# Splitting the projection weights of the second attention at other steps of a head

## The chip, the cores and the metric

The program runs on one core of one Trainium2 chip. The metric is the device time of one execution in microseconds; the median of three runs is given.

## The reference

Two encoder layers over 1024 frames of 1024 features, in float32. Layer 0 uses differential attention with 8 heads, layer 1 latent attention (MLA) with 16 heads; each is followed by a squared-ReLU MLP. The change lies in layer 1's attention: queries come from a 512-wide latent, keys and values from a 256-wide one, 32 of a head's 96 query features are rotated by position, and block t of 128 queries sees the keys up to its own block.

```python
def _rms_norm(x, w):
    xf = x.astype(F32)
    y = xf * lax.rsqrt(jnp.mean(xf * xf, axis=-1, keepdims=True) + RMS_EPS)
    return (y * w.astype(F32)).astype(x.dtype)
...
def mla_attention(u, pos, w_down, q_norm_w, w_uq, kv_norm_w, w_ukv, w_o):
    B, S, _ = u.shape
    down = u @ w_down
    c_q = _rms_norm(down[..., :MLA_Q_LORA], q_norm_w)
    c_kv = _rms_norm(down[..., MLA_Q_LORA:MLA_Q_LORA + MLA_KV_LORA], kv_norm_w)
    k_rope = _rope(down[..., MLA_Q_LORA + MLA_KV_LORA:][:, :, None, :], pos)[:, :, 0]
    q = (c_q @ w_uq).reshape(B, S, MLA_HEADS, MLA_NOPE + MLA_ROPE)
    q_nope = q[..., :MLA_NOPE]
    q_rope = _rope(q[..., MLA_NOPE:], pos)
    kv = (c_kv @ w_ukv).reshape(B, S, MLA_HEADS, MLA_NOPE + MLA_V)
    k_nope, v = kv[..., :MLA_NOPE], kv[..., MLA_NOPE:]
    scale = (MLA_NOPE + MLA_ROPE) ** -0.5
    outs = []
    for qb in range(S // Q_BLOCK):
        q0 = qb * Q_BLOCK
        n_keys = q0 + Q_BLOCK
        s = (jnp.einsum('bqhd,bkhd->bhqk', q_nope[:, q0:n_keys], k_nope[:, :n_keys])
             + jnp.einsum('bqhr,bkr->bhqk', q_rope[:, q0:n_keys], k_rope[:, :n_keys])).astype(F32) * scale
        p = _masked_softmax(s, _chunk_mask(q0, n_keys)[None, None])
        outs.append(jnp.einsum('bhqk,bkhe->bqhe', p.astype(v.dtype), v[:, :n_keys]))
    o = jnp.concatenate(outs, axis=1)
    return o.reshape(B, S, MLA_HEADS * MLA_V) @ w_o
...
    for i in range(DEPTH):
        ...
            y = mla_attention(u, pos, mla_w_down[j], mla_q_norm_w[j], mla_w_uq[j],
                              mla_kv_norm_w[j], mla_w_ukv[j], mla_w_o[j])
        x = _layer_norm(DEEPNORM_ALPHA * x + (1.0 + g1) * y, ln_g[i, 0], ln_b[i, 0])
        u = x * (1.0 + sc2) + sh2
        y = squared_relu_mlp(u, ffn_w1[i], ffn_w2[i])
        x = _layer_norm(DEEPNORM_ALPHA * x + (1.0 + g2) * y, ln_g[i, 1], ln_b[i, 1])
```

## The kernel before

Every float32 product is made of three matmuls in a reduced float format: both operands are held as a high part (the value rounded to the format) and a low part (what is left), and high x high, high x low and low x high are added (`SPLIT`). Activations are kept split. Weights come from HBM by DMA into one of two slots of `raw` and are split there: ScalarE copies the slot into the high half of `W` (`split_hi`, L683), VectorE subtracts that from `raw` and writes the low half (`split_lo`, L1102). Weights have a running number g; its parity is the slot. PE waits for `w_lo`, the count of finished splits, before a product. ScalarE waits for the DMA and for PE to be done with the slot; SyncE loads the next slab into a slot of `raw` when its `w_lo` is reached.

The second attention takes its 16 heads one after another, heads 0 and 1 and heads 14 and 15 written out, heads 2 to 13 as six turns of a loop with two heads each. All engines walk through `heads1(h0, i, last)`, which has eight steps s = 0 to 7, one for each block of 128 queries; they are called the first to the eighth step below, and heads are numbered from 0. Their order of work is written out by hand in this function, once for each engine, and semaphores tie the engines together.

In step s of head h PE turns the exponentials of block s (`turn1`, L1658, 128x128 transposes into `TB` or the bank PA1), makes the scores of the block two steps on (`scores1`, L1980), and in odd s one piece of the next head's projections (`proj1`, by `product`, L1651): queries for the first 512 frames (s = 1, 12 matmuls), keys and values for the first 512 (s = 3, 6 matmuls), queries (s = 5) and keys and values (s = 7) for the second 512. All four pieces use one PSUM bank, `PA[0]`, so that each waits until VectorE has emptied the one before (`qk_evac`). In s = 2, 4, 6 and at the start of the next head it makes the value products of a pair of blocks (`values1`, L2013, then two transposes, L2016). In s = 0 it also turns the values of the head (`turn_v`, L2000 and L1658).

ScalarE makes the exponentials (`exp1`, L1028), the high parts of the turned blocks (`p_hi`, `v_hi`, L729) and of the projections (`copy_piece`, L1019 and L1021), and copies outputs (L1042, L769). VectorE takes row maxima (`max1`, L1566), reciprocals (`inverse1`, L1572), low parts of turned blocks (`p_lo`, `v_lo`, L1184) and of projections (`lo_piece`: L1549 for keys; L1556, L1557 and L1559 for queries), and finishes outputs (`sum_out`: L1586, L1588, then L1230). GpSimd rotates the queries (`rope_q`, L652 to L654), on `tmp`, when VectorE has written it (L1557). SyncE stores outputs and loads weights: in head h the query weights (512 rows, with two small loads of swapped columns) and the key and value weights (256 rows) of head h + 2.

The weights of head h + 1 are split during head h: the query weights (512 columns of `W`) in the first step, the key and value weights (256 columns) in the third, each as the last operation of that step on ScalarE and on VectorE:

```python
                    if proj and s == 0:
                        split_lo(g0, 2 * i, QT)
                    if proj and s == 2:
                        split_lo(g0 + 1, 2 * i, KVT)
```

`proj` is true for heads 0 to 14. `values1` waits for VectorE's earlier outputs (`o_fin`), for the reciprocals, and for the low parts of all blocks it reads (`t_evac`):

```python
                pe.wait_ge(a1["o_fin"], 4 * h + pair)
                pe.wait_ge(a1["l_inv"], NQ * h + last + 1)
                pe.wait_ge(a1["t_evac"], 13 * h + group_of(last, 1 if last >= 4 else 0) + 1)
```

Of the kernel before, what the change touches and what calls it, by code (L numbers as in the profile page):

```python
# [36 lines left out]
QT, KVT = Q_LORA // P, KV_LORA // P  # L37
# [49 lines left out]
def group_of(s, part):  # L87

    return part + (0 if s == 0 else s + 1 + max(0, s - 4))


def is_first(h):

    return isinstance(h, int) and h == 0
# [29 lines left out]
def encoder(nc, x, c, pos_offset, ada_w, ada_b, ln_g, ln_b, rel_table, w_qkv, w_o0, lq1, lk1, lq2,  # L124
# [3 lines left out]
    with ctx:  # L128
# [547 lines left out]
        def _(act):  # L676
            def split_hi(g0, hi, kt, products, count):

                slot = g0 % 2
                act.wait_ge(w_in[slot], 16 * (g0 // 2 + hi + 1))  # L680
                if products is not None:
                    act.wait_ge(products, count)
                nc.scalar.activation(W[:, slot, 0, 0:kt * P], raw[:, slot, 0:kt * P], ACT.Copy).then_inc(w_hi, 1)  # L683
# [81 lines left out]
            def out_hi(s, h, pair, rows, src):  # L765
                act.wait_ge(s["o_fin"], 4 * h + pair + 1)
                if not (isinstance(h, int) and h == 0 and pair == 0):
                    act.wait_ge(s["o_stored"], 16 * (4 * h + pair))
                nc.scalar.activation(ostage[0:rows, 0, :].bitcast(F32R), src, ACT.Copy).then_inc(s["o_hi"], 1)  # L769
# [180 lines left out]
            def split_uq(g0, hi, h, products, count):  # L950
                act.wait_ge(swap_in[0], 32 * h + 64)
                split_hi(g0, hi, QT, products, count)
# [58 lines left out]
            a1 = HS[1]  # L1011
# [32 lines left out]
            def heads1(h0, i, last=False):  # L1044
                h, p = h0 + 2 * i, h0 % 2
                proj = not (last and h0 % 2)
                g0 = G_HEADS1 + 2 * (h0 + 1)
                for s in range(NQ):
                    if s + 1 < NQ:
                        exp1(h, s + 1)  # L1050
                    elif proj:
                        exp1(h + 1, 0)
                    if s == 1:
                        v_hi(h, p)
                    p_hi(h, p, s, 0)
                    if s >= 4:
                        p_hi(h, p, s, 1)
                    if s == 0 and not is_first(h):
                        copy_piece(p, h, 3, PA[0])
                    if s in (2, 4, 6) and proj:  # L1060
                        copy_piece(1 - p, h + 1, s // 2 - 1, PA[0])
                    if s == 1 and not is_first(h):
                        out_bottom(h - 1, 3)
                        out_hi(a1, h - 1, 3, VD, osum[0:VD, :])
                    if s in (3, 5, 7):
                        out_bottom(h, (s - 3) // 2)
                        out_hi(a1, h, (s - 3) // 2, VD, osum[0:VD, :])
                    if proj and s == 0:
                        split_uq(g0, 2 * i, h + 1, a1["pj_ready"], 4 * h + 3)
                    if proj and s == 2:  # L1070
                        split_hi(g0 + 1, 2 * i, KVT, a1["pj_ready"], 4 * h + 4)
                    if not proj and s == 0:
                        split_hi(G_WO1, 0, KT, a1["pj_ready"], 4 * HEADS1)

# [20 lines left out]
        def _(dve):  # L1095
            own = Seq(dve, dve_seq)

            def split_lo(g0, hi, kt):

                slot = g0 % 2  # L1100
                dve.wait_ge(w_hi, g0 + 2 * hi + 1)
                nc.vector.tensor_tensor(W[:, slot, 1, 0:kt * P], raw[:, slot, 0:kt * P],  # L1102
                                        W[:, slot, 0, 0:kt * P].bitcast(F32), ALU.subtract).then_inc(w_lo, 1)
# [438 lines left out]
            a1 = HS[1]  # L1542
# [40 lines left out]
            def sum_out(h, pair):  # L1583
                dve.wait_ge(a1["o_sq"], 4 * h + pair + 1)
                dve.wait_ge(a1["o_lo"], 4 * h + pair)
                nc.vector.tensor_tensor(osum[0:VD, :], VB[0:VD, 0:PAIR], obot[0:VD, :], ALU.add).then_inc(a1["o_sum"], 1)  # L1586
                dve.wait_ge(a1["o_sum"], 4 * h + pair + 1)
                nc.vector.tensor_tensor(osum[0:VD, :], osum[0:VD, :], VB[0:VD, PAIR:2 * PAIR], ALU.mult)\  # L1588
                    .then_inc(a1["o_fin"], 1)
                out_lo(a1, h, pair, VD, osum[0:VD, :])  # L1590

            def heads1(h0, i, last=False):
                h, p = h0 + 2 * i, h0 % 2
                proj = not (last and h0 % 2)
                g0 = G_HEADS1 + 2 * (h0 + 1)
                for s in range(NQ):
                    inverse1(h, s)
                    if s == 1:
                        v_lo(h, p)
                    p_lo(h, p, s, 0)  # L1600
                    if s + 2 < NQ:
                        max1(h, s + 2)
                    elif proj:
                        max1(h + 1, s + 2 - NQ)
                    if s >= 4:
                        p_lo(h, p, s, 1)
                    if s == 0 and not is_first(h):
                        lo_piece(p, h, 3, PA[0])
                    if s in (2, 4, 6) and proj:
                        lo_piece(1 - p, h + 1, s // 2 - 1, PA[0])  # L1610
                    if s == 1 and not is_first(h):
                        sum_out(h - 1, 3)
                    if s in (3, 5, 7):
                        sum_out(h, (s - 3) // 2)
                    if proj and s == 0:
                        split_lo(g0, 2 * i, QT)
                    if proj and s == 2:
                        split_lo(g0 + 1, 2 * i, KVT)
                    if not proj and s == 0:
                        split_lo(G_WO1, 0, KT)  # L1620

# [22 lines left out]
        def _(pe):  # L1644
# [311 lines left out]
            a1 = HS[1]  # L1956
# [48 lines left out]
            def values1(h, pair):  # L2005
                last = 2 * pair + 1
                pe.wait_ge(a1["o_fin"], 4 * h + pair)
                pe.wait_ge(a1["l_inv"], NQ * h + last + 1)
                pe.wait_ge(a1["t_evac"], 13 * h + group_of(last, 1 if last >= 4 else 0) + 1)
                for j in range(last + 1):  # L2010
                    c0 = 0 if j < last else P
                    for b in (1, 0):
                        ins = mm(VB[:, c0:PAIR], V1[:, j, :], at1(pair)[:, b, j, c0:PAIR], start=j == 0 and b == 1,  # L2013
                                 stop=j == last and b == 0)
                for k in range(2):
                    ins = nc.tensor.transpose(VB[0:VD, PAIR + k * P:PAIR + (k + 1) * P],  # L2016
                                              row_inv(2 * pair + k).to_broadcast([P, VD]), ident)
                ins.then_inc(a1["o_ready"], 1)
# [94 lines left out]
```

## Time and profile before

| | |
|---|---|
| median of 3 runs | 3080.66 us (3074.52 to 3080.73) |
| profiled execution | 3074.19 us |
| its span | 3072.5 us |
| PE busy | 2708.4 us, 88% of the span |
| VectorE (DVE) busy | 1689.0 us, 55% |
| ScalarE (ACT) busy | 1184.6 us, 39% |
| GpSimd (POOL) busy | 336.0 us, 11% |
| mean granted PE clock | 0.949 of full speed |

Busy times are of the whole span, which has several stages: setup and the first attention, its output product, the first MLP, the latents, the second attention (from about 1704 to about 2220 us), its output product, the second MLP and the end. The profile names instructions by engine and line, the chain is the work that ended last followed back, and a wait is put down to the engine that released it. Durations of neighbouring instructions on VectorE and ScalarE overlap by some hundredths of a microsecond, so that the distance from one start to the next is a little shorter than the duration.

### The profile page before, as it was taken

Reading aid. Unit: us, or ns where it says so; the run is one execution under the profiler, and the core shown is the slowest. Engines: PE = TensorE matmul, PEld = TensorE weight load, DVE = VectorE, ACT = ScalarE, POOL = GpSimd, SP = SyncE. Lnnn points to the kernel's source line nnn. Section 1 sums busy time; section 2 is a strip of 40 time slices with the busy share of each in tenths; the row PEclk is TensorE's granted clock in tenths of the full one; section 3 lists DMA queues with packets and bytes.
Section 4 is the critical chain, followed back from the end, with each engine's and each line's share of the span. In section 5 each row is a group of like instructions: output and inputs, shape, how many; then the busy total and the mean of one; then the engine's idle time right before and its main releaser. Section 6 shows DMA issues by size and latency. Waiting matters only on the chain.

```text
span 3072.5 us, 37975 instructions
## 1 busy us (share of the span) xinstructions
PE 2708.4 (88%) x12716; PEld 2231.9 (73%) x12716; DVE 1689.0 (55%) x2888; ACT 1184.6 (39%) x2125; POOL 336.0 (11%) x362
## 2 busy tenths in 40 slices
PE   1678878887999999999998788888789999999996
PEld 1566666665778888888776677777567888888884
DVE  3466666665575444354375777777558323232346
ACT  0355555554262120312255565665426212131223
POOL 2000000000020001016032322222101000000000
PEclk9789998886999999999999999999899999999997
DMA  6422222223434324142233111111353211111122
GB/s 195 143 68 73 70 69 66 64 59 145 150 95 130 103 69 135 44 129 61 71 115 86 21 32 27 27 32 26 128 159 86 77 48 48 48 48 48 48 82 76
DMA packets 331200, 245.78 MB, mean 80 GB/s; under 512 B 41000, under 2 KB 303447, under 8 KB 331103
## 3 DMA queue, kind: packets, MB, share of 16 engines
q1 hardware_dynamic: 314062, 185.82, 20.7%
q0 software_dynamic: 17040, 58.73, 6.3%
q8 instruction: 53, 0.87, 0.1%
q14 instruction: 45, 0.36, 0.0%
HBM read 215.12 MB, written 33.59 MB: 81 GB/s over the span
## 4 chain that ended last, share of the span: by engine, by line
PE 63%; DVE 13%; ACT 10%; issue 9%; DMA 4%; ACTq 0%; DVEq 0%; POOL 0%; SPq 0%; POOLq 0%
PE PA L1651 31%; PE SC L1651 24%; PE VB L1739 3%; DVE H L1184 2%; DVE soft L1566 2%; ACT H L729 2%; ACT X L745 2%; DMA ada<-in_ada_w 1%; DVE W L1102 1%; ACT X L1028 1%; ACT W L683 1%; PE TB L1658 1%; DVE H L1223 1%; ACT H L723 1%; DVE X L1588 1%
## 5 line engine op out<-in xcount | busy, mean ns | idle before, releaser
L1651 PE MATMUL PA<-U,W 128*128 128x512 f32 x3840 | 948.8, 402 | 80.8 <-DVE W L1102 46.9
L1651 PEld LDWEIGHTS PA<-U,W 128*128 128x128 f32 x3840 | 730.6, 192 | 245.5 <-issue 57.7
L683 ACT ACTIVATE W<-raw 128x1024 fp32r<-128x1024 f32 (+2 forms) x262 | 259.8, 992 | 830.9 <-PE PA L1651 389.9
L1651 PE MATMUL SC<-U,W 128*128 128x512 f32 x2064 | 484.2, 394 | 4.4 <-DVE W L1102 4.2
L1651 PEld LDWEIGHTS SC<-U,W 128*128 128x128 f32 x2064 | 389.5, 189 | 91.5 <-DVE W L1102 5.9
L1102 DVE TENSOR_TENSOR W<-raw,W 128x1024 fp32r<-128x1024 f32 (+2 forms) x262 | 313.8, 1198 | 99.6 <-ACT W L683 97.9
L1651 PE MATMUL PA<-H,W 128*128 128x512 f32 x1536 | 358.7, 393 | 3.2 <-DVE W L1102 3.2
L1651 PE MATMUL SC<-H,W 128*128 128x512 f32 x1536 | 354.4, 390 | 0.0
L1651 PEld LDWEIGHTS PA<-H,W 128*128 128x128 f32 x1536 | 288.6, 189 | 64.3 <-DVE W L1102 3.6
L1651 PEld LDWEIGHTS SC<-H,W 128*128 128x128 f32 x1536 | 288.5, 188 | 60.5 <-issue 1.0
L729 ACT ACTIVATE H<-TB 128x512 fp32r<-128x512 f32 (+3 forms) x216 | 107.8, 499 | 217.0 <-PE TB L1658 215.6
L1184 DVE TENSOR_TENSOR H<-TB,H 128x512 fp32r<-128x512 f32 (+3 forms) x216 | 122.5, 567 | 122.2 <-ACT H L729 121.8
L1350 DVE SCALAR_TENSOR_TENSOR X<-PA,aff,X 128x512 f32 (+1 forms) x80 | 60.0, 750 | 211.3 <-PE PA L1651 211.3
L1350 DVE SCALAR_TENSOR_TENSOR X<-SC,aff,X 128x512 f32 (+1 forms) x80 | 60.0, 750 | 202.4 <-PE SC L1651 190.1
L524 POOL DMA_DIRECT2D ada<-in_ada_w x96 | 68.8, 717 | 918.8 <-DVE acc L1116 914.3
L1658 PE MATMUL TB<-cst,X 128*128 128x128 f32 (+1 forms) x712 | 124.7, 291 | 48.8 <-DVE H L1184 31.1
L1739 PE MATMUL VB<-H 128*128 128x256 f32 (+1 forms) x480 | 92.8, 371 | 69.9 <-DVE H L1184 69.6
L1739 PEld LDWEIGHTS VB<-H 128*128 128x128 f32 x480 | 90.3, 284 | 74.4 <-DVE H L1184 39.9
L1658 PEld LDWEIGHTS TB<-cst,X 128*128 128x128 f32 (+1 forms) x712 | 86.7, 150 | 74.8 <-issue 21.8
L1980 PE MATMUL SC<-H 104*128 104x512 f32 (+3 forms) x576 | 140.3, 372 | 0.0
L1116 DVE SCALAR_TENSOR_TENSOR acc<-ada,cact,acc 128x512 f32<-128x512 f32 x168 | 125.9, 750 | 23.7 <-DMA ada<-in_ada_w 19.5
L1436 DVE SCALAR_TENSOR_TENSOR tmp<-PA,tmp 128x512 f32<-128x512 f32 x64 | 44.2, 691 | 169.7 <-ACT tmp L892 169.7
(209 smaller groups left out, 2984.1 us busy)
## 6 DMA issues: line engine op xcount, KB each, us to landing
raw<-in_ffn_w SPq DMA_DIRECT2D x160, 512.0 KB, 4.1
ada<-in_ada_w POOLq DMA_DIRECT2D x96, 512.0 KB, 4.7
U<-attention_out SPq DMA_DIRECT2D x4, 3584.0 KB, 17.4
raw<-in_da_w_qkv SPq DMA_DIRECT2D x24, 512.0 KB, 4.2
attention_out<-ostage SPq DMA_DIRECT2D x32, 256.0 KB, 2.7
raw<-in_da_w_o SPq DMA_DIRECT2D x16, 512.0 KB, 4.1
X<-residual SPq DMA_DIRECT2D x4, 2048.0 KB, 11.6
attention_out<-ostage SPq DMA_DIRECT2D x64, 128.0 KB, 2.3
```

Source lines behind the costliest of these rows:

```text
L524: pool.dma_start(ada[:, u % 2, :, :], src[:, 2 * u:2 * u + 2, bass.ds(b * BW, BW)]).then_inc(ada_in[u % 2], 16)
L683: nc.scalar.activation(W[:, slot, 0, 0:kt * P], raw[:, slot, 0:kt * P], ACT.Copy).then_inc(w_hi, 1)
L729: nc.scalar.activation(hi_dst, src, ACT.Copy).then_inc(s["t_hi"], 1)
L745: nc.scalar.activation(w, w, ACT.Exp, bias=st[:, 4 + comp:5 + comp], accum_out=st[:, 6 + comp:7 + comp]).then_inc(a0["p_ready"], 1)
L1102: nc.vector.tensor_tensor(W[:, slot, 1, 0:kt * P], raw[:, slot, 0:kt * P], W[:, slot, 0, 0:kt * P].bitcast(F32), ALU.subtract).then_inc(w_ ...
L1116: ins = nc.vector.scalar_tensor_tensor(acc[:, :], src, by, acc[:, :], ALU.mult, ALU.add)
L1184: nc.vector.tensor_tensor(dst, src, hi_ap.bitcast(F32), ALU.subtract).then_inc(s["t_evac"], 1)
L1350: nc.vector.scalar_tensor_tensor(tile, bank, by, tile, ALU.mult, ALU.add).then_inc(d_evac, 1)
L1651: ins = mm(bank, W[:, slot, a, kt * P:(kt + 1) * P], moving(b, kt)[:, cols], start=kt == first and (a, b) == SPLIT[0], stop=kt == last and ...
L1658: return nc.tensor.transpose(out_ap, in_ap, ident[r0:r0 + n, r0:r0 + n])
L1739: ins = mm(VB[:, c0:PAIR], V0[:, a, j, :], AT0[:, b, j, c0:PAIR], start=j == 0 and (a, b) == SPLIT[0], stop=j == last and (a, b) == SPLIT[-1])
L1980: ins = mm(SC[s % 2][:, k], q1(p, a)[0:MR.stop, s * P:(s + 1) * P], k1(p, b)[0:MR.stop, k], start=(a, b) == SPLIT[0], stop=(a, b) == SPLIT ...
```

## The change

On ScalarE and VectorE alike, in the second attention:

- the key and value weights of the next head are split in the first step instead of the third;
- the query weights are split in the seventh step, two heads ahead: in head h those of head h + 2, in heads 0 to 13;
- head 0 in addition splits the query weights of head 1 in its first step, as before.

ScalarE's copy in the seventh step waits for the two swapped loads of that slab and for the second query product of head h + 1, which PE made in the sixth step. On PE, `values1` waits for the low parts in two portions: for blocks 0 to 3 ahead of the first matmul, for blocks 4 to 7 ahead of the fifth block. No operation is added or left out but these waits: the sequence of splits as such, by number, is the same, and SyncE's instructions are the same.

```diff
--- before.py
+++ after.py
@@ -1065,10 +1065,12 @@
                     if s in (3, 5, 7):
                         out_bottom(h, (s - 3) // 2)
                         out_hi(a1, h, (s - 3) // 2, VD, osum[0:VD, :])
+                    if is_first(h) and s == 0:
+                        split_uq(g0, 2 * i, h + 1, a1["pj_ready"], 4 * h + 3)
                     if proj and s == 0:
-                        split_uq(g0, 2 * i, h + 1, a1["pj_ready"], 4 * h + 3)
-                    if proj and s == 2:
                         split_hi(g0 + 1, 2 * i, KVT, a1["pj_ready"], 4 * h + 4)
+                    if not last and s == 6:
+                        split_uq(g0 + 2, 2 * i, h + 2, a1["pj_ready"], 4 * h + 7)
                     if not proj and s == 0:
                         split_hi(G_WO1, 0, KT, a1["pj_ready"], 4 * HEADS1)
 
@@ -1612,10 +1614,12 @@
                         sum_out(h - 1, 3)
                     if s in (3, 5, 7):
                         sum_out(h, (s - 3) // 2)
+                    if is_first(h) and s == 0:
+                        split_lo(g0, 2 * i, QT)
                     if proj and s == 0:
-                        split_lo(g0, 2 * i, QT)
-                    if proj and s == 2:
                         split_lo(g0 + 1, 2 * i, KVT)
+                    if not last and s == 6:
+                        split_lo(g0 + 2, 2 * i, QT)
                     if not proj and s == 0:
                         split_lo(G_WO1, 0, KT)
 
@@ -2006,8 +2010,9 @@
                 last = 2 * pair + 1
                 pe.wait_ge(a1["o_fin"], 4 * h + pair)
                 pe.wait_ge(a1["l_inv"], NQ * h + last + 1)
-                pe.wait_ge(a1["t_evac"], 13 * h + group_of(last, 1 if last >= 4 else 0) + 1)
                 for j in range(last + 1):
+                    if j % 4 == 0:
+                        pe.wait_ge(a1["t_evac"], 13 * h + group_of(last, j // 4) + 1)
                     c0 = 0 if j < last else P
                     for b in (1, 0):
                         ins = mm(VB[:, c0:PAIR], V1[:, j, :], at1(pair)[:, b, j, c0:PAIR], start=j == 0 and b == 1,
```

What this does to VectorE's order, shown for head 1, which is written out. In the changed kernel VectorE's line numbers are 2 higher. The third step before, from the row maxima of block 4 on (L1566):

```order
L1566 TENSOR_REDUCE soft<-SC 128x1
L1556 SCALAR_TENSOR_TENSOR tmp<-PA,ada 32x512
L1557 SCALAR_TENSOR_TENSOR tmp<-PA,ada 32x512
L1559 SCALAR_TENSOR_TENSOR H<-PA,H 64x512
L1102 TENSOR_TENSOR W<-raw,W 128x256
L1572 RECIPROCAL soft<-soft 128x1
L1184 TENSOR_TENSOR H<-PA,H 128x4x128
```

and now:

```order
L1558 SCALAR_TENSOR_TENSOR tmp<-PA,ada 32x512
L1559 SCALAR_TENSOR_TENSOR tmp<-PA,ada 32x512
L1561 SCALAR_TENSOR_TENSOR H<-PA,H 64x512
L1574 RECIPROCAL soft<-soft 128x1
L1186 TENSOR_TENSOR H<-PA,H 128x4x128
L1568 TENSOR_REDUCE soft<-SC 128x1
```

The split has gone from between L1559 (now L1561) and the reciprocal that opens the fourth step. The seventh step's end and the eighth step before:

```order
L1556 SCALAR_TENSOR_TENSOR tmp<-PA,ada 32x512
L1557 SCALAR_TENSOR_TENSOR tmp<-PA,ada 32x512
L1559 SCALAR_TENSOR_TENSOR H<-PA,H 64x512
L1572 RECIPROCAL soft<-soft 128x1
L1184 TENSOR_TENSOR H<-TB,H 128x4x128
L1566 TENSOR_REDUCE soft<-SC 128x1
L1184 TENSOR_TENSOR H<-PA,H 128x4x128
L1586 TENSOR_TENSOR X<-VB,X 64x256
L1588 TENSOR_TENSOR X<-X,VB 64x256
```

and now:

```order
L1558 SCALAR_TENSOR_TENSOR tmp<-PA,ada 32x512
L1559 SCALAR_TENSOR_TENSOR tmp<-PA,ada 32x512
L1561 SCALAR_TENSOR_TENSOR H<-PA,H 64x512
L1104 TENSOR_TENSOR W<-raw,W 128x512
L1574 RECIPROCAL soft<-soft 128x1
L1186 TENSOR_TENSOR H<-TB,H 128x4x128
L1568 TENSOR_REDUCE soft<-SC 128x1
L1186 TENSOR_TENSOR H<-PA,H 128x4x128
L1588 TENSOR_TENSOR X<-VB,X 64x256
L1590 TENSOR_TENSOR X<-X,VB 64x256
```

The split of 512 columns now stands between the same two kinds of operation as the one of 256 did in the third step. The first step's end, before and now:

```order
L1184 TENSOR_TENSOR H<-PA,H 128x128
L1566 TENSOR_REDUCE soft<-SC 128x1
L1549 TENSOR_TENSOR H<-PA,H 64x512
L1102 TENSOR_TENSOR W<-raw,W 128x512
L1572 RECIPROCAL soft<-soft 128x1
L1184 TENSOR_TENSOR H<-TB,H 128x8x64
```

```order
L1186 TENSOR_TENSOR H<-PA,H 128x128
L1568 TENSOR_REDUCE soft<-SC 128x1
L1551 TENSOR_TENSOR H<-PA,H 64x512
L1104 TENSOR_TENSOR W<-raw,W 128x256
L1574 RECIPROCAL soft<-soft 128x1
L1186 TENSOR_TENSOR H<-TB,H 128x8x64
```

There 256 columns are split in place of 512. ScalarE's order changes in the same way: its copy stands last in the same steps.

## Rows read from the trace of the kernel before

**Rows 1.** Page, part 4: the chain that ended last, by engine.

```profile
PE 63%; DVE 13%; ACT 10%; issue 9%; DMA 4%; ACTq 0%; DVEq 0%; POOL 0%; SPq 0%; POOLq 0%
```

**Rows 2.** Waits, 1736 to 2180 us: engine, line, waited for; total us, times, longest.

```profile
PE PA L1651 <- DVE W L1102: 33.2, 14, 2.5
...
PE PA L1651 <- DVE H L1559: 15.8, 14, 1.2
```

**Rows 3.** Chain that ended last, 1928 to 1993 us: start us, us, what.

```profile
1969.25 1.22 DVE W L1102
...
1988.83 0.42 DVE X L1588
```

**Rows 4.** Timeline of PE, one head: start us, us, instruction, [idle before].

```profile
1957.86 2.11 PE L2013 MATMUL VB<-H 128*128 128x256 f32 x16 [0.25 <-DVE X L1588]
...
1960.39 0.60 PE L1658 MATMUL PA<-cst,X 64*128 64x64 f32 x7
...
1970.60 1.65 PE L1651 MATMUL PA<-U,W 128*128 128x512 f32 x6 [2.34 <-DVE W L1102]
```

**Rows 5.** Timeline of DVE, the same head.

```profile
1960.80 0.67 DVE L1102 TENSOR_TENSOR W<-raw,W 128x512 fp32r<-128x512 f32 x1
...
1969.25 1.22 DVE L1102 TENSOR_TENSOR W<-raw,W 128x256 fp32r<-128x256 f32 x1
1970.39 0.14 DVE L1572 RECIPROCAL soft<-soft 128x1 f32<-128x1 f32 x1
...
1986.81 0.14 DVE L1572 RECIPROCAL soft<-soft 128x1 f32<-128x1 f32 x1
...
1988.83 0.41 DVE L1588 TENSOR_TENSOR X<-X,VB 64x256 f32<-64x256 f32 x1
...
1992.41 0.67 DVE L1102 TENSOR_TENSOR W<-raw,W 128x512 fp32r<-128x512 f32 x1
```

**Rows 6.** Timeline of ACT, the same head.

```profile
1960.07 0.62 ACT L683 ACTIVATE W<-raw 128x512 fp32r<-128x512 f32 x1
1960.59 0.56 ACT L1028 ACTIVATE X<-SC,soft 128x384 f32<-128x384 f32 x1
...
1961.14 0.58 ACT L729 ACTIVATE H<-PA 128x512 fp32r<-128x512 f32 x1
...
1966.23 0.41 ACT L683 ACTIVATE W<-raw 128x256 fp32r<-128x256 f32 x1
...
1989.36 0.42 ACT L769 ACTIVATE ostage<-X 64x256 fp32r<-64x256 f32 x1 [2.87 <-DVE X L1588]
```

**Rows 7.** Timeline of POOL, the same head.

```profile
1968.69 1.50 POOL L652 TENSOR_TENSOR H<-tmp 32x512 fp32r<-32x512 f32 x1 [10.07 <-DVE tmp L1557]
...
1986.25 1.26 POOL L652 TENSOR_TENSOR H<-tmp 32x512 fp32r<-32x512 f32 x1 [13.29 <-DVE tmp L1557]
```

**Rows 8.** Groups of DVE by form, 1700 to 2222 us.

```profile
L1102 DVE TENSOR_TENSOR W<-raw,W 128x256 fp32r<-128x256 f32 x15 | 18.3, 1220 | 0.0
...
L1102 DVE TENSOR_TENSOR W<-raw,W 128x1024 fp32r<-128x1024 f32 x1 | 1.2, 1226 | 0.3 <-ACT W L683 0.3
```

**Rows 9.** Timeline of DVE, head 0, first and third step.

```profile
1706.28 1.14 DVE L1102 TENSOR_TENSOR W<-raw,W 128x512 fp32r<-128x512 f32 x1
...
1712.81 0.56 DVE L1184 TENSOR_TENSOR H<-PA,H 128x384 fp32r<-128x384 f32 x1 [3.32 <-ACT H L729]
```

**Rows 10.** Timeline of POOL, head 0, first step.

```profile
1705.60 1.27 POOL L654 TENSOR_TENSOR H<-tmp,H 32x512 fp32r<-32x512 f32 x1
```

**Rows 11.** Windows of 1 us: us, busy by engine, PEclk, DMA share, GB/s.

```profile
1782.30:1783.30 1.00, 1.00 (x6) 1.00 (x5) 0.44 (x3) 0.84 (x2) 0.21 (x1) 0.50 0.00 0
```

**Rows 12.** Timeline of DVE, first-step split of a later head.

```profile
2024.23 0.67 DVE L1102 TENSOR_TENSOR W<-raw,W 128x512 fp32r<-128x512 f32 x1
```

**Rows 13.** Timeline of PE, heads 10 and 15.

```profile
2034.02 2.92 PE L1651 MATMUL PA<-U,W 128*128 128x512 f32 x6 [2.33 <-DVE W L1102]
...
2217.41 3.68 PE L2013 MATMUL VB<-H 128*128 128x256 f32 x16 [2.18 <-DVE X L1588]
```

## The prediction

> **What bounds the kernel now.** I read the page's chain that ended last first. It is PE for 63% of the span [rows 1], but that is a mean over stages, and the change lies in one of them alone, the second attention. So I went to the waits of that stage. Per head PE sits idle 33.2 / 14 = 2.37 us before the first key and value product, until VectorE has written the low part of the weights (L1102), and 15.8 / 14 = 1.13 us before the second such product, until VectorE has emptied the only projection bank (L1559) [rows 2]. A reader who stops here sees 2.4 us of PE per head to be won. The chain cut to this stage says otherwise: it runs over VectorE and ScalarE, and both the split of the third step and the last VectorE operation of the eighth, L1588, are links of it [rows 3]. PE waits at both ends; it does not set the pace.
>
> One head takes 1992.41 - 1960.80 = 31.61 us from first-step split to first-step split [rows 5]. What must be seen in the three timelines: the third-step split delays VectorE by 1970.39 - 1969.25 = 1.14 us [rows 5] and PE starts only behind it [rows 4]. After the seventh step's L1559, VectorE goes on at 1986.81 and runs without a gap to L1588 at 1988.83 [rows 5]; ScalarE has then been idle for 2.87 us and starts at once when L1588 is done [rows 6], and so does PE with the last value product [rows 4]. Everything of the next head hangs on that moment. So a split put behind L1559 in the seventh step delays the next head by its full length.
>
> **The change, part by part**, against the profiled execution (3074.19 us, of which 3072.5 is span; it lies 6.5 us under the median of the three runs, and I carry the difference over to the median).
>
> Third step, heads 0 to 14: the 256-column split goes away. VectorE is 1.14 us earlier from there on, and the softmax work behind it (L1184, L1566, L1586, L1588) finds its inputs ready. PE gains about as much, not 2.37, since the bank is free only after L1559, which stands right ahead of the split. 15 x -1.14 = **-17.1 us**.
>
> First step, heads 1 to 14: 256 columns are split in place of 512. ScalarE's copy of 512 pushes the next operation back by 1960.59 - 1960.07 = 0.52 us; that of 256 is 0.62 - 0.41 = 0.21 shorter [rows 6]. Only part of that counts: L729 at 1961.14 needs the value transposes, which PE ends at 1960.39 + 0.60 = 1960.99 [rows 4]. With some 0.04 us for the hand-over, 0.11 us are left. The bounds are 0 and 0.21; I take 0.11, since the ends are near each other. 14 x -0.11 = **-1.5 us**. In head 0 both splits stand in the first step; the second one costs nothing on the path, because VectorE has 3.32 us to spare two steps on, where ScalarE and PE are late [rows 9]. Without that cover it would cost about 0.3 us, once.
>
> Seventh step, heads 0 to 13: the 512-column split comes behind L1559. ScalarE's half (0.52 us) delays its exponential of the next head, but VectorE is held much longer and ends last. The low half is an operation with two inputs in SBUF, and GpSimd works at the same moment. In the third step GpSimd's L652 starts at 1968.69 and the split 0.56 us behind it; the split of 256 columns takes 1.22 us there [rows 5, 7], 15 times out of 15 [rows 8], against 0.67 for 512 columns where GpSimd rests [rows 5]. In the seventh step the new split would start at 1986.81, again 0.56 us behind an L652, at 1986.25 [rows 5, 7]: the same geometry. 256 columns more cost (1.23 - 0.67) / 2 = 0.28 us [rows 5, 8], so I expect 1.14 + 0.28 = 1.42 us of delay. Below, 0.60 us would be the price if nothing held it (0.67 less the overlap of some 0.07 that the third-step rows show between length and step); above, 1.14 + 2 x 0.28 = 1.70 if the held part grows with the columns as well. I take 1.42, built on the row with the same neighbour at the same distance. 14 x 1.42 = **+19.9 us**.
>
> A rule speaks here too. Head 0's first-step split shows the holding: it takes 1.14 us and ends at 1707.42, 0.55 us behind the end of L654 at 1706.87 [rows 9, 10]. The Trainium skill (SBUF — State Buffer, Who interferes with whom) says that a VectorE instruction with two SBUF inputs and a GpSimd instruction that reads SBUF take turns, and that whoever came first keeps the shared port for its whole instruction. By that the new split would end 0.55 us behind an L652 of 1.26 us, a delay of 0.70 + 0.55 - 0.08 = 1.17 us, and the sum would come out 14 x 0.25 = 3.5 us lower. Head 0 agrees with the rule, the third step doesn't quite: there L652 itself grows to 1.50 us and the split ends 0.24 us later than in turn [rows 5, 7]. The row decides for me.
>
> The divided wait in the value products: I cost it at nothing. On VectorE each L1588 stands behind both halves of the same step's weights, and PE waits for L1588 (its count of finished outputs) at the head of the same function. So the early half never lets PE start earlier. It adds two waits a head to PE; if each took 0.03 us on the path it would be 14 x 0.03 = 0.4 us for the one that matters. The DMAs keep their order on SyncE; the query weights are issued in the second step of a head and are needed five steps on, and the load of the key and value weights is no longer held until the third step.
>
> PE's clock: in eight of the 15 heads the product after the 2.4 us wait runs partly at the lower level (granted 0.50, that is 1.2 GHz [rows 11]; 2.92 us against 1.65 [rows 4, 13]), and such a head takes 2024.23 - 1992.41 = 31.82 us [rows 5, 12], 0.21 more. The idle time there shrinks to about 1.2 us, and no fall follows the waits of 1.13 us in the old seventh step. I take 8 x -0.21 = **-1.7 us**; the other bound is 0.
>
> Sum: -17.1 - 1.5 + 19.9 - 1.7 = **-0.4 us**: the stall moves from the third step to the turn of the head, and the price is about the same. 3080.66 - 0.4 = **3080.2 us**. About 0.2% (6.2 us) is what a measurement of this kernel can tell from no change.
>
> **Rivals.**
> The split is not held in the seventh step, or the third-step gain is larger than I see: at 0.60 us of delay the sum falls by 14 x 0.82 = 11.5 us, to 3069. For it: GpSimd shows only 1.26 us for this L652. Against it: the distance of 0.56 us is fixed by the same three VectorE operations. If VectorE's eighth step had slack after all, the whole seventh-step term would go, and the time would be near 3060; the gapless run to L1588 speaks against that.
>
> The clock falls at the turn of the head (the slower side). PE now waits 1.1 us for L1559, then about 0.4 for the weights of the eighth step, then about 1.1 for L1588: some 2.6 of 5.2 us idle, where the old third step had 2.4 in one piece. If the clock falls there, it hits the value product, behind which the transposes have only 0.04 us of slack left. The row at the lower level is 3.68 against 2.11 us [rows 4, 13], so 1.6 us per fall. In 7 of 14 heads that is +11 us: 3091. It decides from the fifth such head on. For it: in the last head, where PE has no projections and many waits, that product did run at the lower level [rows 13]. Against: each piece is shorter than the 1.13 us pieces that did no harm.
>
> The held part doubles (1.70): 14 x 0.28 = +3.9 us, 3084, no change that can be told.
>
> The change does nothing at all for PE: that can't be, the splits do change places.
>
> **How the numbers follow.** My forecast, no change, with the doubled holding and the rule's 3.5 us in it: 0.55. Split not held, or slack in the eighth step: 0.24, faster. Clock at the turn, with what else of waiting I miss: 0.21, slower. The forecast's own range is 3075 to 3086 (the rule's and the doubled price, with the scatter of the runs). To leave out no more than 2 in 10 it must reach to both neighbours: 3068 to 3091. Faster by over 0.2%: 0.24; within: 0.55; slower: 0.21.
>
> **What would show it.** Right: PE's wait before the first key and value product falls to about 1.2 us and is put down to L1559; the 512-column split takes about 1.5 us in 14 heads, with L652 at 1.5 us before it; PE waits some 1.1 us for L1588 ahead of the last value product and 0.4 us ahead of the first transposes of the next head; a head takes 31.4 to 31.9 us. Wrong: seventh-step splits of 0.67 us, heads under 31.2 us, or a granted clock of 0.50 in the value product that opens a head.

## The result and the profile after

| | before | changed |
|---|---|---|
| median, 20 runs each | 3074.05 us | 3088.94 us |
| lowest and highest | 3062.27 to 3086.77 | 3072.55 to 3098.81 |
| profiled execution, its span | 3074.19, 3072.5 | 3079.43, 3077.7 |
| mean granted PE clock | 0.949 | 0.952 |

The ratio is 1.0052, 95% interval 1.0038 to 1.0065: **slower**, by about 16 us (12 to 20). The forecast was no change: -0.4 us against before, whose median of 20 runs is 3074.05 in place of the 3080.66 of three.

The stage of the change, from head 0's first-step split to head 15's split of 1024 columns, took 476.53 us before and takes 485.73 us now: +9.2 us. The two profiled spans differ by only 5.2 us, because what lies ahead of the stage was 4 us shorter in that execution: the stage began at 1702.26 us and not at 1706.28. So +9.2 us is what the trace of one execution shows inside the stage, and 16 us is the difference of the medians.

First the waits of PE in the second attention, heads 1 to 14, changed kernel, as in [rows 2]:

```profile
PE PA L1655 <- DVE H L1561: 29.1, 27, 1.2
PE VB L2018 <- DVE X L1590: 13.3, 14, 1.0
PE TB L1662 <- DVE H L1186: 12.4, 21, 0.8
PE PA L1662 <- DVE H L1186: 11.7, 20, 0.7
```

The 33.2 us on the split are gone, and both key and value products now wait 1.0 to 1.1 us for the bank. New are 13.3 us ahead of the value products (1.8 before) and longer waits ahead of the transposes (3.1 and 3.1 before). The four groups sum to 66.5 us; the same four and the split summed to 57.0 us before. So the wait that PE lost has come back at other places, and more than that.

Next the turn of one head, timelines of VectorE and GpSimd, to be held against [rows 5, 7]:

```profile
1954.64 0.68 DVE L1561 SCALAR_TENSOR_TENSOR H<-PA,H 64x512 fp32r<-64x512 f32 x1
1955.25 1.77 DVE L1104 TENSOR_TENSOR W<-raw,W 128x512 fp32r<-128x512 f32 x1
1956.95 0.15 DVE L1574 RECIPROCAL soft<-soft 128x1 f32<-128x1 f32 x1
...
1958.98 0.41 DVE L1590 TENSOR_TENSOR X<-X,VB 64x256 f32<-64x256 f32 x1
...
1962.55 0.41 DVE L1104 TENSOR_TENSOR W<-raw,W 128x256 fp32r<-128x256 f32 x1
```

```profile
1954.69 1.78 POOL L652 TENSOR_TENSOR H<-tmp 32x512 fp32r<-32x512 f32 x1 [12.43 <-DVE tmp L1559]
1956.55 1.60 POOL L653 TENSOR_TENSOR tmp<-tmp 32x512 f32<-32x512 f32 x1
1958.23 1.26 POOL L654 TENSOR_TENSOR H<-tmp,H 32x512 fp32r<-32x512 f32 x1
```

The split stands where it was expected, 0.56 us behind the start of an L652, but it takes 1.77 us, in 14 heads of 14 (1.77 or 1.78), and delays VectorE by 1956.95 - 1955.25 = 1.70 us. L652 takes 1.78 us, not the 1.50 that I expected.

And PE at the turn of a head; the first fence is a head like most, the second one of four:

```profile
1955.38 1.67 PE L1655 MATMUL PA<-U,W 128*128 128x512 f32 x6 [1.13 <-DVE H L1561]
1957.74 0.33 PE L1662 MATMUL TB<-cst,X 128*128 128x128 f32 x1 [0.69 <-DVE H L1186]
1957.83 0.77 PE L1984 MATMUL SC<-H 104*128 104x384 f32 x3
1959.62 2.12 PE L2018 MATMUL VB<-H 128*128 128x256 f32 x16 [1.02 <-DVE X L1590]
```

```profile
1857.82 1.66 PE L1655 MATMUL PA<-U,W 128*128 128x512 f32 x6 [1.13 <-DVE H L1561]
1860.18 0.33 PE L1662 MATMUL PA<-cst,X 128*128 128x128 f32 x1 [0.70 <-DVE H L1186]
1860.26 0.77 PE L1984 MATMUL SC<-H 104*128 104x384 f32 x3
1861.96 3.21 PE L2018 MATMUL VB<-H 128*128 128x256 f32 x16 [0.93 <-DVE X L1590]
```

The windows of 1 us around the second (us, PE busy, PEclk, DMA share, GB/s) show why its value product takes 3.21 us:

```profile
1861.00:1862.00 1.00, 0.07 (x2) 1.00 0.00 0
1862.00:1863.00 1.00, 1.00 (x7) 0.79 0.00 0
1863.00:1864.00 1.00, 1.00 (x6) 0.50 0.00 0
...
1865.00:1866.00 1.00, 1.00 (x5) 0.50 0.00 0
1866.00:1867.00 1.00, 1.00 (x11) 1.00 0.00 0
```

After three pieces of idle time PE is granted 0.50, 1.2 GHz, for more than 3 us. This happens at 1732.57, 1861.96, 1991.62 and 2121.23 (3.44, 3.21, 3.13 and 3.06 us). From split to split in the seventh steps, heads take 31.97 to 32.09 us, on average the 32.05 of the table below, but 33.47 to 33.50 where the clock falls (and 33.18 in the first of the four, in a head that is 0.3 us shorter). The loop's two heads differ by 0.11 us, and the falls lie in the one of 31.97: 1.50 us per fall. The products of the third step, eight of which fell before, are all at 1.60 to 1.67 us.

So the stage adds up to 0.3 us: -17.1 - 1.5 + 14 x 1.70 - 1.7 + 4 x 1.50 = 9.5, against 9.2. That is arithmetic on one trace so far; the runs below take its terms apart.

### The profile page after: what moved, and what is told of

It is laid out like the page before. It is cut to its first block, busy times and chain, and to the rows that moved or that the text cites. A ratio compares the mean times of both kernels' runs of the same rounds, so it can differ in the third digit from the quotient of the medians.

```text
span 3077.7 us, 37999 instructions
## 1 busy us (share of the span) xinstructions
PE 2707.6 (88%) x12716; PEld 2224.5 (72%) x12716; DVE 1693.5 (55%) x2888; ACT 1182.0 (38%) x2125; POOL 343.9 (11%) x362
## 4 chain that ended last, share of the span: by engine, by line
PE 62%; DVE 14%; ACT 10%; issue 9%; DMA 4%; ACTq 0%; DVEq 0%; POOL 0%; SPq 0%; POOLq 0%
PE PA L1655 31%; PE SC L1655 24%; PE VB L1743 3%; DVE H L1186 2%; DVE soft L1568 2%; ACT H L729 2%; DVE W L1104 2%; ACT X L745 1%; DMA ada<-in_ada_w 1%; ACT X L1028 1%; PE TB L1662 1%; ACT W L683 1%; DVE H L1225 1%; DVE X L1590 1%; ACT H L723 1%
## 5 line engine op out<-in xcount | busy, mean ns | idle before, releaser
L1118 DVE SCALAR_TENSOR_TENSOR acc<-ada,cact,acc 128x512 f32<-128x512 f32 x168 | 126.0, 750 | 23.8 <-DMA ada<-in_ada_w 19.8
```

Source lines behind the costliest of these rows:

```text
L1118: ins = nc.vector.scalar_tensor_tensor(acc[:, :], src, by, acc[:, :], ALU.mult, ALU.add)
```

## The experiments

The theory after the result: (a) VectorE's split is held by GpSimd for longer than I took, its columns counting twice; (b) the broken idle time at the turn lets the clock fall; (c) the rest is as forecast. Rivals: the divided wait costs something; the place in the seventh step costs something whatever GpSimd does; ScalarE's part is what counts. The table has each run against before measured alongside it; "stage" is the stretch above in the run's own profiled execution, less the 476.53 us of before, "usual head" is a head without a fall, and "falls" are value products of a turn above 2.9 us in that trace, of 14. A ratio of 1.001 is 3.07 us. The stage of one and the same kernel can differ by 0.9 us (e3 and e11).

| run | ratio, 95% | stage, us | usual head, us | falls |
|---|---|---|---|---|
| changed | 1.0052 [1.0038, 1.0065] | +9.2 | 32.05 | 4 |
| e4, changed again | 1.0036 [1.0016, 1.0057] | +9.3 | 32.05 | 4 |
| e1, undivided wait | 1.0028 [1.0009, 1.0047] | +16.0 | 32.05 | 8 |
| e6, filled waits | 1.0013 [0.9996, 1.0030] | +4.7 | 32.05 | 0 |
| e7, split ahead of L1558 | 0.9995 [0.9976, 1.0014] | -3.0 | 31.03 | 3 |
| e10, split in halves | 0.9992 [0.9973, 1.0012] | -4.4 | 31.46 | 0 |
| e9, third step undone | 1.0112 [1.0085, 1.0139] | +33.4 | 33.35 | 7 |
| e5, little rotation | 0.9966 [0.9947, 0.9984] | -11.8 | 30.95 | 0 |
| e2, both in first step | 0.9950 [0.9932, 0.9968] | -14.2 | 30.78 | 0 |
| e3, split in eighth step | 0.9927 [0.9903, 0.9951] | -19.8 | 30.33 | 0 |
| e11, e3 again | 0.9931 [0.9906, 0.9956] | -20.6 | 30.33 | 0 |
| e8, splits in idle gaps | 0.9941 [0.9916, 0.9967] | -22.2 | 30.33 | 0 |

**e1, the wait in one piece.** The changed kernel with the old line in `values1`:

```diff
+                pe.wait_ge(a1["t_evac"], 13 * h + group_of(last, 1 if last >= 4 else 0) + 1)
                 for j in range(last + 1):
-                    if j % 4 == 0:
-                        pe.wait_ge(a1["t_evac"], 13 * h + group_of(last, j // 4) + 1)
```

> The changed kernel with the undivided wait put back in the value products; the splits stay where the change put them. Theory A (the split of 512 columns is held by GpSimd in the seventh step, 1.77 us in place of 0.67, and PE's clock falls at the turn of some heads, 1.4 us each): nothing moves, heads of 32.05 us where the clock stays up, about 33.5 where it falls, 10 to 20 us slower than before. Theory B (the second wait of a value product, with its register work among the matmuls, is what costs): heads fall back by 0.3 us or more and the time to within 5 us of before.

3081.21 us. The splits take 1.77 us and the usual head 32.05 us, as in the changed kernel, and PE sits idle 0.93 to 1.03 us ahead of nearly every value product in both. The divided wait neither costs nor gains anything on the path. The program is 9 us slower than before (3 to 14), just under the 10 to 20 expected. New is that eight turns fell in this trace: the work on the path is the same, and the number of falls is not.

**e4, the changed kernel once more.**

> The changed kernel itself once more, on the same chip as the others, for a second trace of it. Theory A: the split takes 1.77 us in every head again and a head without a fall 32.05 us; the number of heads whose value product runs at 1.2 GHz differs from the 4 or 5 of the first trace, and the time differs with it by 1.4 us each. If the number of falls is the same and the time isn't, falls are not what spreads the runs.

3081.07 us, four falls and the same stage to 0.1 us, yet a span of 3089.2 us against 3077.7. The 11.5 us between these two executions lie ahead of the stage, which begins at 1702.26 us in one and at 1713.71 in the other. So in these traces falls are not what spreads the spans most, a single span says little here, and the stage says more. The same holds for all traces: the stage begins at 1694 to 1695 (e6, e10), 1702 to 1707 (before, changed, e3, e5, e7, e9, e11) or 1714 to 1716 us (e1, e2, e4, e8), and what follows it takes the same time to 1.7 us. What makes the three levels stays open.

**e2, both splits in the first step.** The kernel before with `if proj and s == 2:` taken out on both engines, so that the key and value split stands right behind the query split.

> The kernel before, with the key and value weights split in the first step right behind the query weights of the same head, and nothing two heads ahead. Theory A: VectorE saves 1.14 us in the third step and pays 0.34 in the first (ScalarE 0.31), where GpSimd rests, so heads take about 30.8 to 31.0 us in place of 31.61 and the program 9 to 12 us less than before; PE's wait before the first key and value product falls from 2.4 to 1.0 us. Theory C (the stage is bound elsewhere, and taking a split off the third step gives nothing by itself): no change within 3 us.

3057.99 us, 15 us faster (10 to 21), where 9 to 12 were expected: the sum for it had left out that no third-step product falls any more. The third-step stall is real and can be won: the head falls from 31.61 to 30.78 us and the two splits together take 1.01 us. PE's wait ahead of the first key and value product falls to 1.35 to 1.6 us, not to 1.0.

**e5, little for GpSimd to do.** The changed kernel, where `rope_q` rotates 16 of each piece's 512 columns and leaves the rest out (the rotated rows are zeroed once, at the start):

```diff
-                    cols = slice(n * HALF, (n + 1) * HALF)
-                    a, b, hi = rows(rope_a(n)), rows(rope_b(n)), q1(p, 0)[KR, cols]
+                    cols = slice(n * HALF, n * HALF + 16)
+                    a, b, hi = rows(rope_a(n))[:, 0:16], rows(rope_b(n))[:, 0:16], q1(p, 0)[KR, cols]
```

> The changed kernel with GpSimd's rotation of the queries cut to 16 of each 512 columns (the others keep zero in the rotated rows; the output is another one). All instructions, waits and their order stay. Theory A (GpSimd's instructions hold the split): the 512-column split of the seventh step takes 0.67 us in place of 1.77, heads take 30.9 to 31.1 us where the clock stays up, PE waits 0.3 us or less for L1590 ahead of the last value product, no or few falls, and the program takes 8 to 12 us less than before. Theory B (the split is slow for another reason, its operands or the neighbouring VectorE operations): 1.77 us again, heads of 32.05 us.

3061.65 us. VectorE in the seventh step (its lines are one higher here):

```profile
1948.20 0.71 DVE L1105 TENSOR_TENSOR W<-raw,W 128x512 fp32r<-128x512 f32 x1
1948.84 0.15 DVE L1575 RECIPROCAL soft<-soft 128x1 f32<-128x1 f32 x1
```

GpSimd's first instruction of the same piece, and of a piece with no split behind it:

```profile
1947.64 0.72 POOL L653 TENSOR_TENSOR H<-tmp 32x16 fp32r<-32x16 f32 x1 [15.62 <-DVE tmp L1560]
...
1962.23 0.21 POOL L653 TENSOR_TENSOR H<-tmp 32x16 fp32r<-32x16 f32 x1 [12.95 <-DVE tmp L1560]
```

The split: same place, same neighbours on VectorE, 0.71 us instead of 1.77. GpSimd's instruction holds the split, not the place. The head is 1.1 us shorter, as the split is. One side expectation missed: PE still waits 0.65 to 0.88 us for the value product, not 0.3 or less.

**e10, the columns.** The split in two instructions of 256 columns, one in the seventh step, one at the end of the eighth:

```diff
-                    if not last and s == 6:
-                        split_lo(g0 + 2, 2 * i, QT)
+                    if not last and s >= 6:
+                        split_half(g0 + 2, 2 * i, s - 6)
```

> The change with VectorE's split of the query weights cut in two: 256 columns at its place in the seventh step, the other 256 at the end of the eighth (where the whole 512 cost nothing on the path). The column law read so far (the held part is the split's columns once as a delay of GpSimd's L652 and once as the split itself) gives for the seventh-step piece 1.22 us, with L652 at 1.50, as in the old third step: a delay of 1.14 us, heads of 30.33 + 1.14 = 31.47 us, against 32.05 in the change. If instead the seventh step is dearer by its place (its price 1.70 not going by columns), the piece takes 1.5 us or more and heads take 31.8 to 32.05. Clock falls: PE's wait ahead of the value product falls from 1.0 to about 0.4 us, so if broken waits make the falls, they go, and the time is 14 x 0.14 = 2 us under the kernel before's, the same within the measurement; if they stay, it is 3 to 6 us above that.

3066.52 us. VectorE, then GpSimd, the same stretch:

```profile
1940.42 1.24 DVE L1112 TENSOR_TENSOR W<-raw,W 128x256 fp32r<-128x256 f32 x1
1941.58 0.14 DVE L1584 RECIPROCAL soft<-soft 128x1 f32<-128x1 f32 x1
...
1944.93 0.41 DVE L1112 TENSOR_TENSOR W<-raw,W 128x256 fp32r<-128x256 f32 x1
```

```profile
1939.86 1.52 POOL L652 TENSOR_TENSOR H<-tmp 32x512 fp32r<-32x512 f32 x1 [12.43 <-DVE tmp L1569]
...
1954.98 1.26 POOL L652 TENSOR_TENSOR H<-tmp 32x512 fp32r<-32x512 f32 x1 [10.86 <-DVE tmp L1569]
```

The piece takes 1.23 or 1.24 us in the 14 heads, as 256 columns did in the old third step, L652 1.52, and the head 31.46 us where 31.47 was expected. The other half costs nothing. My side expectation missed: PE still waits 1.03 us for the value product, since a delay of 1.16 us on VectorE has to appear somewhere in PE's turn. It has less idle time ahead of the transposes instead (0.17 against 0.69), and no turn fell.

**e6, PE kept busy.** The changed kernel makes the scores of two blocks twice, one in the eighth step of a head, one in the first, right where PE waits. No other engine gets more to do.

> The changed kernel in which PE makes the scores twice, with the same result, at the two places ahead of its waits at the turn of a head: those of the next head's second block in the eighth step, ahead of the product that waits for L1561, and those of the third block in the first step, ahead of the value product that waits for L1590. VectorE, ScalarE and GpSimd are untouched. Theory A (PE's idle time at the turn lets the clock fall, and the fall is paid in the value product): no or fewer falls than the 4 to 9 of the three traces of this variant, so heads of 32.05 to 32.15 us and the program 4 to 8 us above before in place of 11 to 16. Theory E (the falls don't depend on what PE does there): as many falls and the same time as the changed kernel, or more, by the added matmuls.

3076.98 us. PE at the turn:

```profile
1946.84 1.65 PE L1655 MATMUL PA<-U,W 128*128 128x512 f32 x6 [0.77 <-DVE H L1561]
1949.20 0.33 PE L1662 MATMUL TB<-cst,X 128*128 128x128 f32 x1 [0.70 <-DVE H L1186]
1949.28 1.29 PE L1984 MATMUL SC<-H 104*128 104x384 f32 x6
1951.08 2.10 PE L2018 MATMUL VB<-H 128*128 128x256 f32 x16 [0.50 <-DVE X L1590]
```

More work for PE, and a shorter stage than in the changed kernel: no fall is left, while the usual head keeps its 32.05 us. This separates the two causes. From head 0's seventh-step split to head 15's split of 1024 columns the traces take 453.61 us here (1722.87 to 2176.48), 459.61 in the changed kernel (1728.38 to 2187.99) and 465.61 in e1 (1742.81 to 2208.42): 0, 4 and 8 falls, 1.50 us each. Without its four falls the changed kernel's +9.2 us would be +3.2. So the held split alone is worth +3.2 to +4.7 us in the stage (the stage up to head 0's seventh step takes 1.5 us more in e6 than in the changed kernel) and about +4 by the runs (-1 to 9); the falls are the rest. The expectation's counts of 4 to 9 fit these only if the last head's value product is counted in, which is slow in every trace (3.45 to 3.68 us).

**e9, one part of the change undone.** The key and value split goes back to the third step; the query split stays in the seventh.

> The change with one part undone: the key and value split goes back from the first to the third step, so that VectorE is held in the third step (256 columns) and in the seventh (512). If the two stalls are independent terms of one path, a head without a clock fall takes what the change's does (32.05 us) plus the third step's 1.14 less the first step's small share (0.11): 33.0 to 33.2 us, the splits take 1.22 and 1.77 us, and the time is some 15 us above the change's with its clock falls, less what falls go away: about 3095 against about 3072 before, ratio 1.006 to 1.010. If instead the third-step stall only fills a wait that the seventh step's makes anyway, heads stay near 32.1 us and the time stays at the change's ratio of 1.003 to 1.005.

3105.27 us, 34 us slower than before. The waits of PE, 1740 to 2150 us:

```profile
PE PA L1655 <- DVE W L1104: 26.8, 12, 2.3
PE PA L1655 <- DVE H L1561: 13.6, 12, 1.2
PE VB L2018 <- DVE X L1590: 11.7, 12, 1.0
```

Both stalls stand side by side, and both add to the head: 33.35 us against 32.05, of which some 0.2 would be the fall in the third step, by its price in the kernel before. They are terms of one path, and neither hides in the other. It came out above the expected 1.006 to 1.010 because the clock fell in the third step of every head from 1 on (2.3 to 2.9 us for a product of 1.65) and in seven turns besides (heads of about 34.9 us).

**e3 and e11, the split at the end of the eighth step.** VectorE's half moves from `s == 6` to `s == 7`; ScalarE's stays in the seventh.

```diff
-                    if not last and s == 6:
+                    if not last and s == 7:
                         split_lo(g0 + 2, 2 * i, QT)
```

> The changed kernel with VectorE's half of the query split moved from the end of the seventh step to the end of the eighth, behind the last output operation of the step; ScalarE's half stays in the seventh. Theory A: GpSimd is done or nearly done there and VectorE has some 0.5 us of slack, so the split takes 0.67 us and lies off the path; heads take 30.4 to 30.6 us, no clock falls at the turn of the head, and the program takes 15 to 19 us less than before. Theory D (what costs is that VectorE has 512 columns to do anywhere between the seventh step and the next head's first): heads of 31.0 us or more, no more than 8 us less than before.

> The version with the query split at the end of the eighth step again, for a better interval: both stalls are gone from VectorE, heads take 30.3 us, no clock falls, and the gain is 15 x 1.3 = 19 us or a little more: ratio 0.992 to 0.995. A rival: the first measurement of 0.9927 from few executions was high, and the whole program gives part of it back: 0.996 or more.

3051.05 and 3052.22 us, 21 to 22 us faster than before (15 to 30 and 14 to 29), better than both kernels and than the 15 to 19 expected of the first. VectorE from L1590 on, in e3:

```profile
1947.82 0.41 DVE L1590 TENSOR_TENSOR X<-X,VB 64x256 f32<-64x256 f32 x1
1948.80 0.68 DVE L1232 TENSOR_TENSOR ostage<-X,ostage 64x256 fp32r<-64x256 f32 x1 [0.56 <-ACT ostage L769]
1949.40 0.67 DVE L1104 TENSOR_TENSOR W<-raw,W 128x512 fp32r<-128x512 f32 x1
1950.01 0.15 DVE L1574 RECIPROCAL soft<-soft 128x1 f32<-128x1 f32 x1
```

Behind L1590 PE and ScalarE have what they wait for, and VectorE may be late. GpSimd's last instruction of that piece, L654, ended at 1949.20, and the split takes 0.67 us. All of the forecast's gains are there (-17.1 - 1.5 - 1.7 = -20.3 us; the stages say -19.8 and -20.6) without the seventh-step price. ScalarE's copy, still in the seventh step, costs nothing (e8, where it moves too, has the same head), so the rival that ScalarE's part is what counts is out.

**e7, the split ahead of L1558.** Still in the seventh step, but before the three operations of `lo_piece`, while GpSimd rests.

> The changed kernel with VectorE's half of the query split moved ahead of its three projection operations in the seventh step, so that it ends before GpSimd's L652 is released. Theory A: it takes 0.67 us, delays L1561 and with it PE's second key and value product by 0.6 us and the turn of the head by 0.6 in place of 1.7; heads of 30.9 to 31.1 us, PE waits about 1.7 us ahead of that product and 0.3 ahead of the value product; 6 to 12 us less than before. Theory B (slow for another reason): 1.77 us again, heads of 32 us or more.

3070.60 us. The split takes 0.69 us in every head, so the holding can be avoided inside the same step. PE and the bank pay instead:

```profile
1888.93 2.90 PE L1655 MATMUL PA<-U,W 128*128 128x512 f32 x6 [1.83 <-DVE H L1561]
```

PE waits 1.83 us in one piece, its clock falls in that product in four heads and in the value product in three, and such heads take 1.05 to 1.1 us more. The usual head is the expected one (31.03 us). The expected gain of 6 to 12 us did not come: the ratio says -7 to +4 us. The seven falls, some 7.5 us, are about what is missing.

**e8, every half in an idle gap.** ScalarE's query copy goes to the eighth step, the key and value split to the second, between operations that wait for others.

> As the variant with VectorE's query split at the end of the eighth step, but with all other halves put where their engine waits anyway: ScalarE's query copy in the eighth step between its two output copies, the key and value split in the second step, ScalarE's copy between its output copies and VectorE's half between the output product and the low part of the output. Theory A: heads of 30.0 to 30.25 us against 30.33, the program 19 to 25 us less than before, 1 to 4 less than that variant. Theory F (the first-step splits were free already): 30.33 us again.

3061.26 us and the same heads as in e3, 30.33 us: the first-step splits were free already. Its 12 runs lie at 3041 to 3043 (four), 3052 and 3061 to 3064 (seven). The stage doesn't explain this. The steps of 10 us are those between the three levels at which the stage begins (under e4): the profiled execution, 3061.03 us, has the latest, 1715.28. For the other runs, which have no trace, that is not shown.

## Why the prediction was wrong

- **Third step, -17.1 us: right.** e9 puts the stall back (and takes 256 columns out of the first step again), and the head grows from 32.05 to 33.35, less some 0.2 for its fall: 1.1 us, where 1.14 less 0.11 was to be expected.
- **First step, -1.5 us: fits, but only in the sum.** With the seventh-step price gone, e3 shows 31.61 - 30.33 = 1.28 us a head, where the two terms give 1.14 + 0.11 = 1.25. No run takes the first step's 0.11 us by itself.
- **Falls of the third step, -1.7 us: right.** Eight before, none now. Head by head the eight cost 1.5 us.
- **Divided wait, nothing: right** (e1).
- **Seventh step, +19.9 us: failed, a term too small.** I added 0.28 us for 256 more columns to the third step's 1.14 and took 1.42. Measured is 1.70, my upper bound, whose reading ("if the held part grows with the columns as well") was the correct one: 14 x 1.70 = 23.8, +3.9 us. The hint was in [rows 7]: L652 had grown there from 1.26 to 1.50 us, by 0.24, just about what 256 columns cost VectorE. I used that row to fix the distance, and didn't ask what its growth would be with twice the columns.
- **The turn's clock, left out of the sum: failed, and the larger half of the miss.** I gave it as the rival that ends slower and argued against it that "each piece is shorter than the 1.13 us pieces that did no harm". The falls came. The pieces did add up: 1.13 + 0.69 + 1.02 us, where I had forecast 1.1, 0.4 and 1.1; the missing 0.3 us is again the held split. The price per fall is 1.50 us against the 1.6 taken. The profiled execution has four falls (+6.0 us), fewer than the "fifth such head" that I named as the point of decision, another has eight. That point moves when the held part is right: with the sum at +3.5 us, two falls just pass 0.2%, and four to eight give +9.5 to +15.5 us. The two measurements of the changed kernel say 16 (12 to 20) and 11 (5 to 17), and e1, which is as good as a third, 9 (3 to 14).

So the split alone is +3.2 to +4.7 us, no change that can be told (e6), and four falls alone would have made -0.4 + 6.0 = 5.6 us, not 0.2% either; together they are slower. The rule weighed in the forecast is the Trainium skill's (SBUF — State Buffer, Who interferes with whom), that the engine that came first keeps the shared port for its whole instruction while the other waits. It gave a delay of 1.17 us. The traces don't agree: the delay is 1.70 us, and the earlier instruction, L652, grows as well. It erred further than the row did, on the same side.

That the kernel could be slower though its worst wait was gone was clear from the chain, and the sum had it: the stall moved to the turn. What I did not do was to price a place that the diff did not use. Behind L1590 the same split costs nothing (e3).

## What to carry to other kernels

An operation that is taken from a place where it costs something pays only if the new place has slack: look for the point behind which nobody waits for the engine (here behind L1590), not for the step that looks empty. Where an instruction is held by another engine, read how both durations grow with size before scaling either. Idle time of PE is to be added up over a stretch with its short pieces: several short waits did what one long one had done. But the sum alone does not settle it: 2.33 us in three pieces made no fall (e10), 1.83 in one piece made seven (e7).

## What the runs showed of the hardware

A VectorE operation with two SBUF inputs that starts 0.56 us into GpSimd's L652 (1.26 us alone) counts its columns twice. With 256 columns L652 takes 1.50 to 1.52 and the split ends 0.28 us behind it; with 512 columns it takes 1.78 and the split ends 0.55 us behind it. The splits thus take 0.70 + 0.24 + 0.28 = 1.22 and 0.70 + 0.52 + 0.55 = 1.77 us, where 0.70 us is what was left of L652. GpSimd's next instruction grows too (L653, 1.60 against 1.28). In e5, where GpSimd's first instruction has 16 columns, it grows by as much: 0.72 us against 0.21 where no split follows, though by its usual length it would have ended before the split began. So the growth goes by VectorE's columns and not by GpSimd's. Why it grows, though it came first, no run here shows.

PE's idle pieces ahead of the value product of a turn, and whether its clock fell: 1.13 + 0.25 us (before and e3: never), 1.83 in one piece, with at most 0.25 behind it (e7: 7, four of them in the projection), 0.77 + 0.70 + 0.50 (e6: never), 1.13 + 0.88 (e5: never), 1.13 + 0.17 + 1.03 (e10: never), 1.13 + 0.69 + 1.02 (changed kernel: 4, 4 and, in e1, 8 of 14), 1.13 + 0.71 + 1.03 (e9: 7). With the same waits, some turns fall and others don't: in the changed kernel and in e4 every fourth, the same four, in e9 every second, in e1 others again. What decides it stays open.
